# Attention stage of an encoder step: when stream keys and bias rows are asked for, and how many first splits precede the first job

## The chip, the cores and the metric

The program runs on one core of one Trainium2 chip. The metric is the device time of one execution, in microseconds (us); lower is better. A core has TensorE (PE: matmuls and transposes, with its weight loads as PEld), VectorE (DVE), ScalarE (ACT), GpSimd (POOL) and SyncE (SP, which here issues nearly all DMAs). Each engine works through its own instructions in order and waits on semaphores for others.

## The reference, cut to what matters

One layer over a prompt of 2048 tokens and over eight running streams of 16 new tokens each, model width 1024, 8 heads of 64 in group A ("fox") and 8 in group B ("band"):

```python
h = rmsnorm(x, norm_mix_pre)
qa, ka, va, logf, qb, kb, vb = project_in(h, w_in, b_forget)
oa = fox_fn(qa, ka, va, logf)      # causal, logit += C[t] - C[s], C = cumsum(logf)
ob = band_fn(qb, kb, vb)           # own chunk of 64 and the 8 before, bias by distance
oa = rmsnorm(oa.reshape(...), gain_out_a)
ob = rmsnorm(ob.reshape(...), gain_out_b)
x = x + rmsnorm(jnp.concatenate([oa, ob], axis=-1) @ w_out, norm_mix_post)
hf = rmsnorm(x, norm_ffn_pre)
x = x + rmsnorm((jax.nn.silu(hf @ w_gate) * (hf @ w_up)) @ w_down, norm_ffn_post)
```

For a stream, group A attends to 1024 cached keys and values and the 16 new ones, group B to 512 cached ones and the new ones. Everything is float32.

## The kernel before, in words

The program has four stages, one after the other: `front` (norm and input projection), `attend`, `mix_out` (output projection) and `feed_forward`. The change touches `attend` alone. All dense products are made of high and low parts (a high part that the matmul takes exactly, and the rest), so a raw block of queries or keys is first split: ACT writes the high part (`split_high`, L1083 on), DVE the low part (`split_low`, L1139 on).

**Jobs.** The stage is a list of 144 jobs (`JOBS`). Jobs 0 to 63 are group A of the prompt: four pairs of heads, 16 query blocks of 128 each, block i against i+1 key tiles. From job 64 (`WIDE`) on come four pairs of group B, 16 blocks each with at most five key tiles, and among them 16 stream jobs, one behind the third of every four band jobs: streams 0 to 7 are group A of the eight running streams (nine key tiles), 8 to 15 group B (five). A stream job thus comes every fifth job: n, n+5, and so on.

**Order.** `attend_order` writes out one order for PE, ACT and DVE: the scores of job n+2 stand among the transposes ("turns") of job n. A job goes: PE scores, in pieces, to two score buffers; DVE adds the bias to a piece and keeps the running minimum (`biased`, L1234; for streams L1203), which frees the score buffer; ACT takes the exponential (L1106); PE transposes (L999, streams L979); ACT and DVE copy out (L1117, L1245); PE multiplies with the values (L1035, streams L1015); DVE copies (`outward`), PE transposes back, DVE normalises (`evict`, L1276), SP stores (L780, streams L777).

**The pair's queries and keys.** A pair has eight raw chunks of 128 x 512, 256 KB each: four of keys (c below 4) and four of queries. They go through three raw buffers; SP asks for chunk x (`load_raw`, L755) when the low split of chunk x-3 has freed the buffer. For pairs 1 to 7 the chunks are asked during jobs 2 to 9 of the pair before and split after jobs 4 to 11. For pair 0, ACT and DVE make all eight splits before the first job, and PE's job 0 waits for the eighth low split (L950). On SP the first three chunks come first, then the two bias rows of the pair (L768, 1 MB each), its values (L761, 1 MB), then the other five chunks, then the bias table of group B (L836, L840), then the loop over jobs.

**Stream constants.** DVE's `stream_consts` (L1150 on) waits for GpSimd's steps on `own` and `fold`, and stands ahead of DVE's first low split. `own` lies in `sx[2][:, 0, 0:512]`, which job 2 overwrites.

**Streams on SP.** Keys of group A come in two halves of 1 MB to `kr[0]` and `kr[1]` (L799), which is the space of the prompt's bias rows `bb[0]`; values likewise to `bb[1]` (L822). The bias rows of a group A stream, `bt[s % 2]` (0.5 MB, L803), are broadcast from `csum`; GpSimd then adds a mask to their last 16 columns (L914), and DVE's first biased piece of the stream waits for that. Group B has one table for all streams (L809). SP's loop does, for each job n, in this order: values and bias rows of the next pair at i = 2 and 3; the queries, keys, bias rows and values of stream 0 at job 64; keys and bias rows of the next stream at a stream job; values of the next stream at the job after it; the store of job n-1 (which waits for its evict); and a raw chunk.

```python
if n == WIDE:
    load_queries()
    load_keys(0)
    load_values(0)
if n in STREAM_AT and p + 1 < NST:
    load_keys(p + 1)
if n - 1 in STREAM_AT and JOBS[n - 1][1] + 1 < NST:
    load_values(JOBS[n - 1][1] + 1)
if n >= 1:
    store(n - 1)
if kind != "stream" and p + 1 < NPAIR and 2 <= i < 10:
    load_raw(8 * (p + 1) + i - 2)
```

A piece of a stream's scores waits for its half of the keys, and from the third piece on (the 16 new keys) for the biased first piece, since two score buffers alternate (L933).

Of the kernel before, what the change touches and what calls it, by code (L numbers as in the profile page):

```python
# [15 lines left out]
SEQ = 2048  # L16
# [623 lines left out]
def attend(nc, t, keep, neg_c):  # L640
# [6 lines left out]
    LMAX = PAST_A + NQ  # L647
    WIDE = PAIR_AT[NPAIR // 2]
    NPT, NSX, NSM, NOS, NRAW = 3, 3, 5, 4, 3
    HALVES = [(s, h) for s in range(NST) for h in range(stream_keys(s) // 4)]  # L650
# [12 lines left out]
    with ExitStack() as ctx:  # L663
# [38 lines left out]
        qb = [sx[2][:, 1, 5 * P + 2 * GW + P * u:5 * P + 2 * GW + P * (u + 1)].rearrange("p (c q) -> p c q", c=CH) for u in range(2)]  # L702
        own = sx[2][:, 0, 0:GW]

# [22 lines left out]
        def splits_at(n):  # L727

            kind, p, i = JOBS[n]
            return [8 * (p + 1) + i - 4] if kind != "stream" and p + 1 < NPAIR and 4 <= i < 12 else []  # L730

        def last_of(n, g):
            return g == len(job_groups(n)) - 1
# [11 lines left out]
        with nc.Block() as block:  # L745

            @block.sync
            def _(sp):
                def load_raw(x):
                    p, c = divmod(x, 8)  # L750
                    base, off = rows(p)
                    r0 = base + off + (GW if c < 4 else 0)
                    if x >= NRAW:
                        sp.wait_ge(s_lo, x - NRAW + 1)
                    sp.dma_start(raw[x % NRAW][:], t["zT"][r0:r0 + P, (c % 4) * 512:(c % 4 + 1) * 512]).then_inc(s_raw[x % NRAW], 16)  # L755
# [33 lines left out]
                def load_keys(s):  # L789
                    band, b = divmod(s, NB)  # L790
                    keys = t["cache_bk"] if band else t["cache_ak"]
                    for h in range(stream_keys(s) // 4):
# [3 lines left out]
                        else:  # L796
                            ps, ph = HALVES[x - 2]
                            sp.wait_ge(s_sc, S0[STREAM_AT[ps]] + ph + 1)
                        sp.dma_start(kr[x % 2], keys[b][:, :, h * 512:(h + 1) * 512]).then_inc(l_k[x % 2], 16)  # L799
                    if band == 0:  # L800
                        if s >= 2:
# [39 lines left out]
                for n in range(NJOB):  # L841
                    kind, p, i = JOBS[n]
                    if kind != "stream" and p + 1 < NPAIR:
                        if i == 2:
                            load_v(p + 1)
                        if i == 3 and fox(p + 1):
                            load_bias(p + 1)
                    if n == WIDE:
                        load_queries()
                        load_keys(0)  # L850
                        load_values(0)
                    if n in STREAM_AT and p + 1 < NST:
                        load_keys(p + 1)
                    if n - 1 in STREAM_AT and JOBS[n - 1][1] + 1 < NST:
                        load_values(JOBS[n - 1][1] + 1)
                    if n >= 1:
                        store(n - 1)
# [59 lines left out]
            def _(pe):  # L917
# [19 lines left out]
                def score(n, g):  # L937
# [10 lines left out]
                    diag = fox(p) and tiles[-1] == i  # L948
                    if i == 0:
                        pe.wait_ge(s_lo, 8 * (p + 1))  # L950
# [131 lines left out]
            def _(act):  # L1082
                def split_high(x):  # L1083
                    p, c = divmod(x, 8)
                    u = p % 2
# [33 lines left out]

                for x in range(8):  # L1120
                    split_high(x)
                for e in range(2):
                    exps(0, e)
                for what, n, g in ORDER:
                    if what == "turn":
# [7 lines left out]
                        if last_of(n, g):  # L1133
                            for x in splits_at(n):
                                split_high(x)

            @block.vector
            def _(dve):
                def split_low(x):  # L1139
                    p, c = divmod(x, 8)  # L1140
                    u = p % 2
# [141 lines left out]
                nc.vector.drain().then_inc(s_cst, 1)  # L1283
                stream_consts()
                for x in range(8):
                    split_low(x)
                held, ended = [], []
                for what, n, g in ORDER:
                    if what == "score":
                        biased(n, g)  # L1290
                    else:
# [13 lines left out]
                        copy(n, g)  # L1305
                        held.append((n, g))
                        if n == WIDE and g == 0:
                            stream_pad()
# [966 lines left out]
```

## Time and profile before

| | |
|---|---|
| median of 3 executions | 3291.67 us (3288.47 to 3296.19) |
| the profiled execution | 3288.23 us, span 3286.5 us |
| PE busy | 2942.9 us (90%) |
| DVE, ACT, POOL busy | 1659.4, 1208.5, 469.6 us |
| mean granted TensorE clock | 0.96 |
| attention stage | about 610 to 1480 us of the span |
| keys of group A streams, asked to landed | 1024 KB each, 8.3 us (median) |
| DMA traffic | 376.37 MB, mean 115 GB/s |

The span is from the first to the last instruction. A timeline row gives the start, the length, the engine, the line of the kernel and the tiles, and in brackets how long the engine was idle before and what released it. A window row gives a stretch "A:B" in us and its length, then the busy time of PE, PEld, DVE, ACT and POOL in it (with the number of instructions), the granted clock (1.00 is 2.4 GHz, 0.50 is 1.2 GHz), the share of time that the 16 DMA engines were busy, and the GB/s moved.

### The profile page before, as it was taken

What the parts mean: (1) busy time and instruction counts of PE and PEld (TensorE: products, weight loads), DVE (VectorE), ACT (ScalarE), POOL (GpSimd) and SP (SyncE); (2) the same over time, 40 slices, a digit from 0 to 9 for tenths busy, and PEclk for the clock granted to TensorE, in tenths of its full rate; (3) what the DMA queues carried; (4) which work ended last, traced back from release to release, by engine and by line L of the source; (5) the groups of instructions that cost most, each with busy time, mean ns of one, the idle gap of its engine ahead of it and who ended that gap; (6) DMA issues with size and microseconds to landing.
All of it is one profiled execution on the core that took longest, in us unless ns stands there. A gap on an engine that the chain in (4) does not pass through costs nothing. (4 is left out here: it accounts for less than half of the span.)

```text
span 3286.5 us, 57063 instructions
## 1 busy us (share of the span) xinstructions
PE 2942.9 (90%) x23073; PEld 2633.0 (80%) x23073; DVE 1659.4 (50%) x3253; ACT 1208.5 (37%) x2124; POOL 469.6 (14%) x402
## 2 busy tenths in 40 slices
PE   7999999688888667787994999999999996998998
PEld 7999999577677445655884999999999994886887
DVE  6222221377666445664445766786676653223444
ACT  5320000266666344553443333433343333223211
POOL 0000000100000000000113544453344320000000
PEclk9999999899999789998996999999999998999999
DMA  5322121412211765434543322333222225434553
GB/s 166 89 78 76 63 72 60 137 39 76 74 36 46 211 201 181 145 112 167 162 141 118 141 104 103 122 107 105 105 87 105 105 79 164 106 93 135 176 176 118
DMA packets 275868, 376.37 MB, mean 115 GB/s; under 512 B 16456, under 2 KB 203864, under 8 KB 263576
## 3 DMA queue, kind: packets, MB, share of 16 engines
q1 hardware_dynamic: 273368, 368.43, 35.3%
q8 instruction: 184, 3.01, 0.4%
q10 hardware_dynamic: 2240, 4.30, 0.4%
q14 instruction: 76, 0.62, 0.1%
HBM read 283.52 MB, written 89.15 MB: 113 GB/s over the span
## 5 line engine op out<-in xcount | busy, mean ns | idle before, releaser
L2064 PE MATMUL dwn_py<-dwn_wh,dwn_ah 128*128 128x512 f32 x748 | 296.9, 397 | 42.0 <-DVE dwn_al L2139 32.6
L1117 ACT ACTIVATE att_pts<-att_pt 128x384 f32<-128x384 f32 (+3 forms) x444 | 207.7, 493 | 284.6 <-PE att_pt L999 255.6
L2065 PE MATMUL dwn_py<-dwn_wl,dwn_ah 128*128 128x512 f32 x748 | 294.1, 393 | 0.0
L2066 PE MATMUL dwn_py<-dwn_wh,dwn_al 128*128 128x512 f32 x748 | 293.9, 393 | 0.0
L1106 ACT ACTIVATE att_sx<-att_sx,att_nm 128x640 f32<-128x640 f32 (+17 forms) x272 | 265.2, 976 | 19.0 <-DVE att_os L1276 17.7
L1035 PE MATMUL att_po<-att_pts,att_vv 128*64 128x128 f32 x3296 | 230.0, 286 | 44.0 <-DVE att_os L1276 38.2
L1035 PEld LDWEIGHTS att_po<-att_pts,att_vv 128*64 128x64 f32 x3296 | 195.0, 144 | 66.2 <-issue 62.1
L999 PEld LDWEIGHTS att_pt<-att_eye,att_sx 64*128 64x128 f32 x3296 | 132.2, 141 | 130.8 <-ACT att_pts L1117 83.1
L79 PE MATMUL frt_pz<-frt_xhi,frt_hi 128*128 128x448 f32 (+1 forms) x640 | 230.5, 360 | 0.0
L81 PE MATMUL frt_pz<-frt_xhi,frt_lo 128*128 128x448 f32 (+1 forms) x640 | 230.5, 360 | 0.0
L80 PE MATMUL frt_pz<-frt_xlo,frt_hi 128*128 128x448 f32 (+1 forms) x640 | 230.1, 359 | 0.0
L999 PE MATMUL att_pt<-att_eye,att_sx 64*128 64x64 f32 x3296 | 171.3, 234 | 65.1 <-ACT att_pts L1117 33.7
L514 DVE TENSOR_TENSOR frt_shared<-frt_pz,frt_rb 128x448 f32<-128x448 f32 (+1 forms) x80 | 48.9, 611 | 313.6 <-PE frt_pz L81 313.6
L2064 PEld LDWEIGHTS dwn_py<-dwn_wh,dwn_ah 128*128 128x128 f32 x748 | 142.3, 190 | 80.6 <-DVE dwn_al L2139 33.7
L79 PE MATMUL frt_pv<-frt_hi,frt_xhi 128*128 128x256 f32 (+1 forms) x544 | 157.2, 289 | 18.6 <-DVE frt_lo L446 15.7
L1779 PE MATMUL gup_z<-gup_hh,gup_wh 128*128 128x362 f32 (+1 forms) x528 | 173.2, 328 | 0.0
L1781 PE MATMUL gup_z<-gup_hl,gup_wh 128*128 128x362 f32 (+1 forms) x528 | 173.2, 328 | 0.0
L1782 PE MATMUL gup_z<-gup_hh,gup_wl 128*128 128x362 f32 (+1 forms) x528 | 172.7, 327 | 0.0
L2066 PEld LDWEIGHTS dwn_py<-dwn_wh,dwn_al 128*128 128x128 f32 x748 | 142.3, 190 | 30.1
L2065 PEld LDWEIGHTS dwn_py<-dwn_wl,dwn_ah 128*128 128x128 f32 x748 | 142.5, 190 | 28.4
L1713 POOL TENSOR_TENSOR gup_tr<-gup_wr 128x512 f32<-128x512 f32 x66 | 88.9, 1347 | 523.7 <-DVE gup_wl L1884 410.1
L80 PE MATMUL frt_pv<-frt_lo,frt_xhi 128*128 128x256 f32 (+1 forms) x544 | 154.3, 284 | 0.0
(251 smaller groups left out, 7473.7 us busy)
## 6 DMA issues: line engine op xcount, KB each, us to landing
gup_wr<-in_w_gu SPq DMA_DIRECT2D x65, 1024.0 KB, 5.1
dwn_ar<-mid_act SPq DMA_DIRECT2D x67, 704.0 KB, 6.0
att_raw<-out_zT SPq DMA_DIRECT2D x64, 256.0 KB, 3.0
att_bb<-in_cache_ak SPq DMA_DIRECT2D x16, 1024.0 KB, 8.3
att_bb<-in_cache_av SPq DMA_DIRECT2D x16, 1024.0 KB, 14.2
mid_act<-gup_ao SPq DMA_DIRECT2D x44, 362.0 KB, 2.5
out_zT<-frt_shared SPq DMA_DIRECT2D x64, 224.0 KB, 1.9
frt_raw<-in_w_slab SPq DMA_DIRECT2D x11, 1024.0 KB, 5.3
```

The costliest lines, as they stand in the source:

```text
L79: nc.tensor.matmul(out, a_hi(k), b_hi(k), start=(k == 0), stop=False)
L80: nc.tensor.matmul(out, a_hi(k), b_lo(k), start=False, stop=False)
L81: last = nc.tensor.matmul(out, a_lo(k), b_hi(k), start=False, stop=(k == kk - 1))
L999: last = nc.tensor.transpose(pt[x][:, to:to + 64], sx[n % NSX][r, e, c:c + P], eye[r, r])
L1035: last = nc.tensor.matmul(po[n % 2][r, 0:P], vv[u][:, kt, r], pts[G % NPT][:, e, j, :], start=(g == 0 and j == 0), stop=(g == len(groups) ...
L1106: nc.scalar.activation(sx[n % NSX][:, e, :w], sx[n % NSX][:, e, :w], ACT.Exp, bias=nm[n % NSX][:, e:e + 1], scale=-1.0, accum_out=sums[n % ...
L1117: nc.scalar.activation(pts[G % NPT][:, :, 0:k, 64 * x:64 * x + 64], pt[x][:].rearrange("p (e j q) -> p e j q", e=2, q=64)[:, :, 0:k, :], A ...
L1779: nc.tensor.matmul(out, high[:, k, :], hh[:, x, k, :w], start=(k == 0 and not more), stop=False, skip_group_check=True)
L1781: nc.tensor.matmul(out, high[:, k, :], hl[:, x, k, :w], start=False, stop=False, skip_group_check=True)
L2064: nc.tensor.matmul(out, ah[u][:, j, :], wh[:, j, :], start=(j == 0), stop=False)
L2065: nc.tensor.matmul(out, ah[u][:, j, :], wl[:, j, :], start=False, stop=False)
L2066: last = nc.tensor.matmul(out, al[u][:, j, :], wh[:, j, :], start=False, stop=(j == NJ - 1))
```

## The change

Six edits, all in `attend`:

- Keys of a stream are asked at the job before the stream job ahead of it (one job sooner), those of stream 0 at job 63 in place of 64.
- The bias rows get a function of their own, `load_table`; those of streams 0 and 1 are asked at job 64 behind the queries, those of stream s+2 at the job after stream s, behind the values of stream s+1.
- The raw chunks of every pair are taken in the order keys 0, queries 0, keys 1, queries 1 and so on (`CHUNKS`).
- Only two chunks are split before job 0; ACT and DVE split two more behind each of jobs 0, 1 and 2 (`first_splits`).
- PE's wait for the low splits of pair 0 is now made in fours: job 0, 4, 8 and 12 wait for 2, 4, 6 and 8 of them.
- `stream_consts` moves behind the first group of job 6 on DVE, and `own` to columns 1536 to 2047 of the second half of `sx[2]`, which no job before 14 writes.

```diff
+    CHUNKS = [0, 4, 1, 5, 2, 6, 3, 7]
-        own = sx[2][:, 0, 0:GW]
+        own = sx[2][:, 1, SEQ - GW:]
+        def first_splits(n):
+            return [2 * n + 2, 2 * n + 3] if n < 3 else []
@@ load_raw, split_high, split_low @@
-                    p, c = divmod(x, 8)
+                    p, c = x // 8, CHUNKS[x % 8]
@@ sync: load_keys, load_table @@
+                def load_table(s):
+                    band, b = divmod(s, NB)
                     if band == 0:
                         if s >= 2:
                             sp.wait_ge(s_bi, 2 * S0[STREAM_AT[s - 2] + 1])
...
+                    if n == WIDE - 1:
+                        load_keys(0)
                     if n == WIDE:
                         load_queries()
-                        load_keys(0)
+                        load_table(0)
+                        load_table(1)
                         load_values(0)
-                    if n in STREAM_AT and p + 1 < NST:
-                        load_keys(p + 1)
+                    if n + 1 in STREAM_AT and JOBS[n + 1][1] + 1 < NST:
+                        load_keys(JOBS[n + 1][1] + 1)
                     if n - 1 in STREAM_AT and JOBS[n - 1][1] + 1 < NST:
                         load_values(JOBS[n - 1][1] + 1)
+                        if JOBS[n - 1][1] + 2 < NST:
+                            load_table(JOBS[n - 1][1] + 2)
@@ tensor: score @@
-                    if i == 0:
+                    if p == 0 and i % 4 == 0:
+                        pe.wait_ge(s_lo, 2 * (i // 4 + 1))
+                    if p > 0 and i == 0:
                         pe.wait_ge(s_lo, 8 * (p + 1))
@@ scalar @@
-                for x in range(8):
+                for x in range(2):
                     split_high(x)
...
                         if last_of(n, g):
-                            for x in splits_at(n):
+                            for x in first_splits(n) + splits_at(n):
                                 split_high(x)
@@ vector @@
-                stream_consts()
-                for x in range(8):
+                for x in range(2):
                     split_low(x)
...
                         held.append((n, g))
+                        for y in first_splits(n):
+                            split_low(y)
+                        if (n, g) == (6, 0):
+                            stream_consts()
```

## Rows read from the trace of the kernel before

**Rows 1.** Waits of all engines, 590 to 1490 us: total, times, longest.

```profile
PE att_s L956 <- DVE att_ql L1147: 25.2, 1, 25.2
...
PE att_s L933 <- DVE att_nm L1203: 20.8, 8, 4.4
...
PE att_s L933 <- DMA att_bb<-in_cache_ak: 20.2, 7, 7.2
...
ACT att_qh L1093 <- DMA att_raw<-out_zT: 18.2, 5, 8.1
```

**Rows 2.** Timeline of the start: start us, us, engine, line, operation, tiles [idle before].

```profile
611.59 0.91 SPq L768 DMA_DIRECT2D att_bb<-mid_neg_c  x2
...
618.60 0.17 DVE L1152 MEMSET att_fc<- 128x128 f32 x1 [4.15 <-POOL att_fold L900]
...
620.72 1.90 DVE L1145 TENSOR_TENSOR att_kl<-att_raw,att_kh 128x512 fp32r<-128x512 f32 x3
...
621.43 6.95 SPq L755 DMA_DIRECT2D att_raw<-out_zT  x5
...
626.02 0.63 ACT L1091 ACTIVATE att_kh<-att_raw 128x512 fp32r<-128x512 f32 x1 [9.18 <-DMA att_raw<-out_zT]
...
633.88 0.29 DVE L1234 CUSTOM_DVE_ANT_0 att_sx<-att_s,att_bb 128x128 f32<-128x128 f32 x1 [1.51 <-PE att_s L962]
```

**Rows 3.** DMA issues from 609 to 613 us: KB each, median us to landing.

```profile
att_bb<-mid_neg_c SPq DMA_DIRECT2D x2, 1024.0 KB, 8.7
...
att_vv<-out_v SPq DMA_DIRECT2D x1, 1024.0 KB, 12.8
```

**Rows 4.** Timeline about streams 0 and 1, the columns as in rows 2.

```profile
1052.46 0.32 SPq L780 DMA_DIRECT2D mid_mixT<-att_os  x1
...
1063.42 1.27 SPq L799 DMA_DIRECT2D att_bb<-in_cache_ak  x2
...
1064.73 0.73 SPq L803 DMA_DIRECT2D att_sx<-mid_csum  x1
...
1080.54 0.22 POOL L914 TENSOR_TENSOR att_sx<-att_sx,att_late 128x16 f32<-128x16 f32 x1 [443.84 <-DMA att_sx<-mid_csum]
...
1090.96 0.43 SPq L761 DMA_DIRECT2D att_vv<-out_v  x1
...
1097.60 1.25 SPq L799 DMA_DIRECT2D att_bb<-in_cache_ak  x2
...
1107.54 1.45 PE L933 MATMUL att_s<-att_bb,att_sx 128*32 128x512 f32 x8 [2.88 <-DMA att_bb<-in_cache_ak]
```

**Rows 5.** Windows of scoring streams 0, 1, 4, 5, 7; sum of 1 to 7.

```profile
1064.20:1081.99 17.79, 4.18 (x28) 0.74 (x28) 2.04 (x9) 1.85 (x6) 0.22 (x1) 0.58 0.99 285
...
1103.59:1113.60 10.01, 3.67 (x38) 1.35 (x40) 1.28 (x4) 2.81 (x7) 0.22 (x1) 0.72 1.05 286
...
1192.58:1200.90 8.32, 2.44 (x28) 0.65 (x32) 0.89 (x3) 1.52 (x6) 0.22 (x1) 0.76 1.00 272
...
1221.23:1231.77 10.54, 4.16 (x38) 1.42 (x40) 1.33 (x4) 2.31 (x6) 0.22 (x1) 0.64 1.05 245
...
1290.97:1294.45 3.48, 2.70 (x42) 1.09 (x40) 1.26 (x4) 2.19 (x6) 0.22 (x1) 1.00 1.06 325
...
sum 48.75, PE 21.30 PEld 7.77 DVE 8.56 ACT 16.95 POOL 1.54; mean PE 3.04 PEld 1.11 DVE 1.22 ACT 2.42 POOL 0.22
```

**Rows 6.** Windows: streams 0 to 8, and four stretches between streams.

```profile
1081.99:1311.48 229.49, 167.06 (x2534) 121.45 (x2533) 118.19 (x457) 106.26 (x264) 1.54 (x7) 0.86 0.65 192
...
1113.60:1140.07 26.47, 21.63 (x310) 17.11 (x311) 15.47 (x60) 12.64 (x30) 0.00 (x0) 0.78 0.52 163
...
1146.26:1171.87 25.61, 20.13 (x310) 15.85 (x310) 16.04 (x61) 12.12 (x29) 0.00 (x0) 0.88 0.58 177
...
1231.76:1257.51 25.75, 20.20 (x311) 15.93 (x311) 15.46 (x60) 13.20 (x32) 0.00 (x0) 0.88 0.56 175
...
1264.07:1290.97 26.90, 20.57 (x310) 15.89 (x310) 16.04 (x61) 12.12 (x29) 0.00 (x0) 0.81 0.56 177
```

More of the change, by code:

```diff
@@ L1083, in split_high @@
                 def split_high(x):
-                    p, c = divmod(x, 8)
+                    p, c = x // 8, CHUNKS[x % 8]
                     u = p % 2
@@ L1139, in split_low @@
                 def split_low(x):
-                    p, c = divmod(x, 8)
+                    p, c = x // 8, CHUNKS[x % 8]
                     u = p % 2
```

## The prediction

> **What bounds the kernel now.** I read the waits of the TensorE queue (PE) over the attention stage first, because PE is the engine that is nearly always at work and its waits say which stalls are long and rare. Three lines stand out [rows 1]: one wait of 25.2 us for the low half of the last query split, eight times the scores of a stream wait for the reduced minimum of the piece before (20.8 us), and seven times they wait for a stream's keys (20.2 us). The rest of PE's waits are short ones between jobs. The change is aimed at these three, so the sum goes over these three places, each read in its own timeline.
>
> The start [rows 2]: the vector engine (DVE) can do no low split until it has built the constants of the streams, and those wait for GpSimd: it goes idle for 4.15 us, starts the constants at 618.60 and the first low split at 620.72. The raw buffers are free only then, so SyncE (SP) asks for the other five chunks from 621.43 on, and the first of them reaches ScalarE (ACT) at 626.02. PE starts behind the last of them, the first biased scores at 633.88. The two bias rows of the first pair (asked at 611.59) land a median of 8.7 us after their issue, and the values after 12.8 us [rows 3].
>
> The first stream [rows 4]: a store is issued at 1052.46, the keys only at 1063.42 and the table of bias rows at 1064.73, behind 2 MB of keys. GpSimd gets the table at 1080.54, and the last piece is scored at 1081.99. PE had left its band work at 1064.20; the window between holds 17.79 us and 4.18 us of matmuls [rows 5].
>
> The next seven streams of group A [rows 5]: the windows from the first key matmul (or the start of the wait for it) to the end of the last piece sum to 48.75 us; those of streams 1, 4, 5 and 7 stand there. The seventh, without a late transfer, takes 3.48 us. The DMA share is 1.00 to 1.06 in them, and 0.52 to 0.58 in the stretches between [rows 6]: transfers stand behind each other just where they are waited for.
>
> The clock [rows 6]: over the 229.5 us from the end of the first stream's scores to the first stream of group B PE was granted 0.86 of full speed, though nothing but the stalls differs: the 3.48 us window has 1.00, the 10.54 us window 0.64.
>
> **The change, part by part.**
>
> (A) First splits. ACT and DVE do two of eight before job 0. DVE's first low split can follow its two casts of constants; PE's scores then wait for nothing but these, at about 616. But the biased step also needs the bias rows, 611.59 and half a microsecond for the second, and 8.7: 620.8. The pipeline so starts 633.88 - 620.8 = 13.0 us sooner. Given back: six splits now stand in ACT's queue, two behind each of jobs 0 to 2, ahead of the next job's copies, which PE waits for. Each takes 0.63 us, so 3.8 us if nothing hides them. The fourth chunk, now asked at about 615, still stands behind the values on SP's one queue; values land at about 625.4, so the chunk at about 626, as now [rows 2, 3], while ACT would come to it near 624.6: 1.4 us more. The later chunks are each asked when a low split frees a buffer, and fit in the same steps. DVE's six low splits (0.69 us each) lie beside ACT's. I take 5.0; bounds 0 (all in the slack of these small jobs) and 11 (ACT's 3.8, DVE's 4.1 and a further 3 of waits for chunks). Moved to job 6: the constants, 620.72 - 618.60 = 2.1 us of DVE; I take half of that on the path, 1.0, bounds 0 and 2.1. The table and far loads of group B come after the eighth chunk, needed 400 us later: nothing. Stores of jobs 0 to 3 wait a little behind them; four output buffers cover that. (A) = 13.0 - 5.0 - 1.0 = 7.0.
>
> (B) First stream. Its keys are asked behind the store at 1052.46, 10.9 us sooner, and have all landed when PE needs them. The queries still wait for the turn of the last group A job and stay where they are; the table goes right behind them, without the 2 MB ahead. No row shows such a table alone. From below, a raw chunk of half the size is used 4.6 us after it was asked [rows 2]; from above, this table took 15.8 us [rows 4]. The nearest rows are the bias rows, broadcast from memory in the same way at twice the size, 8.7 us with chunks before them [rows 3]; at 0.5 MB and with 1 MB of queries partly ahead I take 6, so it lands at 1070. From its landing to the end of the last piece is 1081.99 - 1080.54 = 1.45 us, so the stream's scores end at 1071.5 instead of 1081.99: 10 us (bounds 1 and 12).
>
> (C) Streams 1 to 7. Tables come a whole stream period ahead and can't be late. Keys are asked one job sooner, just behind the store before: for stream 1 right behind the values of the next pair, 1090.96 + 0.5 instead of 1097.60 [rows 4], 6 us sooner. The second half of its keys landed at about 1107.5 [rows 4], so it now comes at 1102 to 1103, delayed a little by the 1 MB in front, against a need one piece (about 1 us) behind 1103.59, less the 1 to 2 us by which the jobs before run faster. Streams 1 and 5 have those values in front; I leave 1.5 us of waits to the two. All seven at the clean 3.6: 48.75 - 25.2 = 23.6, less 1.5: 22 (bounds 18 and 24).
>
> (D) The clock. 229.5 x 0.14 = 32 us of full clock are lost. The three slow scoring windows hold 10.01 x 0.28 + 8.32 x 0.24 + 10.54 x 0.36 = 8.6 of that, which (C) counts already; 23 lie between streams. What they cost I read from two pairs of equal stretches of jobs [rows 6]: 26.47 us at 0.78 against 25.75 at 0.88 is 0.72 us for 2.7 lost, and 26.90 at 0.81 against 25.61 at 0.88 is 1.29 for 2.0: 0.26 and 0.63 us each. At 0.4 it is 9.2; an eighth of it stays for the first stream, which still stalls: 8.0 (bounds 3 and 14). The granted clock is a mix of 1.2 and 2.4 GHz (0.64 to 0.76) in the windows with late transfers, and 2.4 GHz throughout in the one without [rows 5]. The Trainium skill (TensorE: Matmul & The Clock Gate, HAM oscillation) prices a cold stretch at throttled time times one half, so one microsecond for each lost here; by it (D) would be some 20 and the sum 59. The pairs speak against it, because PE waits for ACT and DVE in much of a job and these don't slow down.
>
> (E) No gain: streams 8 to 15. They have half the keys and no wait for them in any row; a sooner request changes nothing. SP meets one wait earlier, for the scores of the stream at hand before the next keys; those are done well before the store ahead of it, so nothing queues behind it.
>
> Sum: 7 + 10 + 22 + 8 = 47 us. The profiled execution took 3288.23 us (span 3286.5), 3.4 below the median of the three, 3291.67. So 3241 for an execution like the profiled one, and 3244.7 against the median: **3245**.
>
> **The rivals.**
>
> R1, the clock pays in full: with the stalls gone PE's steps are the path and each lost microsecond counts one. (D) is 20, the time 3291.7 - 59 = 3233. For it: PE is busy 167 of the 229 us [rows 6]. Against: both pairs. 0.12.
>
> R2, transfers stay in line: the askings are sooner, the landings are not. DMA share 1.04 in each scoring window, on one queue. The waits for keys of streams 1 to 7 stay (of 20.2 us stream 0 has the longest, 7.2, and some more; 10.5 are theirs), half the clock with them (4), and the start pays back what it gained, since its six chunks stand behind 3 MB (7). 47 - 21.5: 3266. Against: between the windows the share is little over half, so an earlier request has room. The Trainium skill (DMA: Bandwidth & Descriptors, Queues, rings and completion order) says that each DMA engine consumes descriptors in ring order; by that, what is asked behind the next pair's values lands behind them, which is this rival. 0.14.
>
> R3, slower: raw chunks behind keys. For three pairs, the chunks of the third and the seventh job are now asked behind 2 MB of keys, and ACT does its splits in order, ahead of copies that PE waits for. ACT's longest wait for a chunk of queries is 8.1 us now, of 18.2 us in five waits [rows 1]. Six such waits of 8.1 are 49 us: the gain is gone, 3293; if the following chunk of each is held by 1.5 more it is 3302. It decides only if each is held over 7.8 us, and a split comes about two jobs, 10 us, after its request. 0.04.
>
> R4, it doesn't do what it says: SP comes to the moved lines no sooner, because the store ahead of them is the late one and every part but the tables falls flat; that is between R2 and no change. 0.03, at 3280.
>
> **How the numbers follow.** Forecast 0.67, R1 0.12, R2 0.14, R3 0.04, R4 0.03. The forecast's own bounds: (A) 0 to 13, (B) 1 to 12, (C) 18 to 24, (D) 3 to 14 would be 22 to 63; they are unlikely to go one way, so 35 to 59 for it: 3233 to 3257. With R1 inside and most of R2: range 3229 to 3266. A measurement of this kernel tells about 0.2% (6.6 us) from no change. Slower by more: R3's upper half and a bit of the unseen, 0.03. Within: 0.03. Faster: 0.94.
>
> **What would show it.** First biased scores at 620 to 622 and job 3 some 7 us sooner than before; the single PE wait of 25 us down to about 12. The waits for the reduced minimum fall from 20.8 to about 8, those for keys from 20.2 to under 3, GpSimd's add for stream 1 on comes many microseconds ahead of DVE. The clock is 1.00 in every window of rows 5 and above 0.95 between. Wrong: ACT waits for raw chunks of over 3 us in groups; keys of streams 1 and 5 still waited for by more than 2 us each; or the clock still 0.5 after streams 1 to 7.

## The result, and where the time went

The changed kernel takes 3267.99 us, median of four runs (3266.86 to 3269.07), the kernel before 3293.02 beside it (four runs, 3288.47 to 3296.19): a ratio of 0.9925, 95% interval 0.9908 to 0.9942. That is 25 us (19 to 30) where 47 were forecast; 3245 was said, and the range ended at 3266. The two profiled executions took 3288.23 and 3266.86, spans of 3286.5 and 3265.1, so the traces show 21.4 of the 25.

The waits of all engines of the changed kernel, 590 to 1490 us (total, times, longest), answer to [rows 1]:

```profile
ACT att_kh L1105 <- DMA att_raw<-out_zT: 115.3, 8, 91.2
...
PE att_pt L1013 <- ACT att_pts L1131: 53.8, 35, 7.5
ACT att_qh L1107 <- DMA att_raw<-out_zT: 39.4, 10, 7.7
...
PE att_s L970 <- DVE att_ql L1161: 9.5, 1, 9.5
PE att_s L970 <- DVE att_nm L1248: 8.6, 11, 3.4
...
PE att_s L945 <- DVE att_nm L1217: 5.5, 1, 5.5
```

The three waits that the change is aimed at fell as forecast or further: the one for the low splits from 25.2 to 9.5, those for the reduced minimum from 20.8 to 5.5, those for a stream's keys from 20.2 to none. In their place stand PE's waits for ACT's copies of the transposes (L1131), which were 33.7 us in 33 waits before, none over 2.6, and are 53.8 now with one of 7.5, and PE's waits for the minimum of a prompt job's piece (L1248), 8.6 for 1.5. ACT's waits for raw chunks did not grow as a whole. Those for chunks of queries went from 18.2 to 39.4, but the chunks now come in another order, so keys and queries have to be taken together: without the one wait of 91 us for the stage ahead they are 68.9 us before and 63.5 now. The line of the keys before, which [rows 1] does not show:

```profile
ACT att_kh L1091 <- DMA att_raw<-out_zT: 142.1, 13, 91.4
```

The windows that answer to [rows 5] (streams 0, 1, 4, 5, 7), then the whole stretch from stream 0 to stream 8 and three stretches between streams, as in [rows 6]:

```profile
1071.45:1079.23 7.78, 2.24 (x26) 0.69 (x28) 0.93 (x3) 0.29 (x2) 0.22 (x1) 0.83 0.88 187
1099.63:1102.68 3.05, 2.63 (x38) 1.06 (x40) 1.88 (x5) 1.74 (x5) 0.00 (x0) 1.00 1.05 397
1185.60:1189.30 3.70, 3.66 (x30) 0.99 (x32) 0.70 (x2) 1.21 (x5) 0.00 (x0) 0.52 1.05 397
1210.60:1213.20 2.60, 2.60 (x42) 1.06 (x38) 1.61 (x4) 1.82 (x5) 0.00 (x0) 1.00 1.05 390
1273.50:1276.20 2.70, 2.70 (x42) 1.12 (x40) 1.67 (x4) 1.36 (x4) 0.00 (x0) 1.00 1.09 404
```

```profile
1079.20:1292.50 213.30, 159.88 (x2532) 116.27 (x2532) 117.82 (x456) 105.82 (x262) 1.54 (x7) 0.89 0.67 212
1102.68:1132.76 30.08, 19.72 (x312) 15.29 (x313) 14.91 (x58) 14.18 (x34) 0.22 (x1) 0.83 0.59 196
1135.40:1164.00 28.60, 19.50 (x314) 15.16 (x318) 15.62 (x61) 13.63 (x33) 0.22 (x1) 0.88 0.58 169
1213.20:1243.30 30.10, 19.25 (x319) 14.92 (x318) 15.17 (x60) 14.21 (x34) 0.22 (x1) 0.89 0.64 186
```

Streams 1 to 7 are scored in 3.0, 2.6, 2.6, 4.4, 2.6, 2.6 and 2.6 us by the trace, 20.4 in all against 48.75; stream 0's window, from PE's last band work to the last piece, has 9.3 us against 17.8. Both terms were met. But the stretch between streams 1 and 2 grew from 26.47 to 30.08 us, that between 2 and 3 from 25.61 to 28.60, that between 5 and 6 from 25.75 to 30.10, with the same matmuls in them and the clock no higher than 0.89.

**The account.** The end of each job's evict in the two traces, after minus before, gives it in stages: at job 4, -1.5 us (where the forecast had -7); at job 62, the last but one of group A, +5.6, so 7.2 lost (forecast none); at job 63, behind stream 0's scores, -3.5, so 9.2 gained (forecast 10); at job 110, past streams 1 to 8, -20.0, so 16.5 gained (forecast 22 + 8); at the last job -21.9. Of the 1.5 us at job 4 the stage ahead has 0.7: the pair's bias rows are asked that much sooner. Three things are to be explained: the 13.5 missing among the streams, the 5.5 missing at the start, and the 7.2 lost in group A.

**Among the streams.** This is SP's queue about stream 1 in the changed kernel, by the timeline (columns as in [rows 2]), and the split that ACT makes of the chunk asked at 1101.16, then PE's next transposes:

```profile
1087.42 0.44 SPq L765 DMA_DIRECT2D att_vv<-out_v  x1
1087.90 2.88 SPq L803 DMA_DIRECT2D att_bb<-in_cache_ak  x2
...
1092.82 1.29 SPq L759 DMA_DIRECT2D att_raw<-out_zT  x1
...
1094.68 1.40 SPq L829 DMA_DIRECT2D att_bb<-in_cache_av  x2
...
1097.78 0.64 SPq L810 DMA_DIRECT2D att_sx<-mid_csum  x1
...
1101.16 0.42 SPq L759 DMA_DIRECT2D att_raw<-out_zT  x1
```

```profile
1111.37 0.63 ACT L1107 ACTIVATE att_qh<-att_raw 128x512 fp32r<-128x512 f32 x1 [7.15 <-DMA att_raw<-out_zT]
```

```profile
1112.32 0.91 PE L1013 MATMUL att_pt<-att_eye,att_sx 64*128 64x64 f32 x12 [7.23 <-ACT att_pts L1131]
```

The chunk takes 10.2 us from its request to its use, behind 2 MB of values and 0.5 MB of bias rows; ACT stands before its split for 7.15 us with the copies that PE needs behind it, and PE stands 7.23. The same happens behind streams 2, 5 and 6 (ACT 5.97, 7.66, 5.42). The kernel before had four such waits as well (6.91, 6.22, 4.46, 8.14); the one behind stream 1 has the same 10.2 us from request to use:

```profile
1108.19 0.42 SPq L755 DMA_DIRECT2D att_raw<-out_zT  x1
```

```profile
1118.45 0.63 ACT L1091 ACTIVATE att_kh<-att_raw 128x512 fp32r<-128x512 f32 x1 [6.91 <-DMA att_raw<-out_zT]
```

Yet PE's waits for ACT's copies in the stretch from stream 0 to stream 8 were 9.1 us before and are 25.9 now:

```profile
PE att_pt L999 <- ACT att_pts L1117: 9.1, 4, 2.6
```

```profile
PE att_pt L1013 <- ACT att_pts L1131: 25.9, 5, 7.5
```

ACT's own waits for chunks in it grew only from 25.8 us to 30.4. What changed is when they fall. Before, PE's stall in the stream's scores gave the chunk time to travel: the four chunks came 4.9, 5.0, 5.0 and 5.7 us after the stream's last score, and PE had work for most of that. Now they come 8.7, 7.5, 9.2 and 7.0 us after it.

### The profile page after: what moved, and what is told of

Its sections match the earlier page's. It is cut to its first block and busy times, and to the rows that moved or that the text cites. A ratio compares the mean times of both kernels' runs of the same rounds, so it can differ in the third digit from the quotient of the medians.

```text
span 3265.1 us, 57072 instructions
## 1 busy us (share of the span) xinstructions
PE 2937.8 (90%) x23073; PEld 2632.7 (81%) x23073; DVE 1661.9 (51%) x3253; ACT 1208.4 (37%) x2124; POOL 470.6 (14%) x402
## 5 line engine op out<-in xcount | busy, mean ns | idle before, releaser
L1131 ACT ACTIVATE att_pts<-att_pt 128x384 f32<-128x384 f32 (+3 forms) x444 | 207.7, 493 | 256.6 <-PE att_pt L1013 227.7
L1013 PE MATMUL att_pt<-att_eye,att_sx 64*128 64x64 f32 x3296 | 171.1, 234 | 88.2 <-ACT att_pts L1131 53.8
```

What stands on the lines that cost most here:

```text
L1013: last = nc.tensor.transpose(pt[x][:, to:to + 64], sx[n % NSX][r, e, c:c + P], eye[r, r])
L1131: nc.scalar.activation(pts[G % NPT][:, :, 0:k, 64 * x:64 * x + 64], pt[x][:].rearrange("p (e j q) -> p e j q", e=2, q=64)[:, :, 0:k, :], A ...
```

## The experiments

Fourteen more runs were made, one of them the changed kernel again, each beside the kernel before on the same chip, which took 3292.6 to 3293.5 us there. All kernels compute the whole reference. The edits are to the kernel before or to the changed one, as each says; times are medians of four or more runs where an interval stands.

**The two halves apart.** e1_streams is the kernel before with the edits to SP's loop alone, e2_start the changed kernel with the old loop, the reverse of the same lines:

```diff
+                    if n == WIDE - 1:
+                        load_keys(0)
                     if n == WIDE:
                         load_queries()
-                        load_keys(0)
+                        load_table(0)
+                        load_table(1)
                         load_values(0)
-                    if n in STREAM_AT and p + 1 < NST:
-                        load_keys(p + 1)
+                    if n + 1 in STREAM_AT and JOBS[n + 1][1] + 1 < NST:
+                        load_keys(JOBS[n + 1][1] + 1)
...
+                        if JOBS[n - 1][1] + 2 < NST:
+                            load_table(JOBS[n - 1][1] + 2)
```

> The kernel before with the stream edits alone (keys a job sooner, bias rows two streams ahead); the start as before. Theory T (the stream edits are worth more than the whole change, the start edits cost time by the end of group A): the changed kernel's last group A jobs come 4 to 6 us late although its first job is evicted 3 us early, so without the start edits 25 + 4 = 29 us are gained: 3264. Rival (the late group A jobs are chance, another phase of the clock, and the start is worth its 2 to 3 us): 3271.

> The changed kernel with the old requests for keys and bias rows: only the start edits are left (two splits before the first job, the order of the chunks, the constants at job 6). Theory T: 3 us gained at the first evict, lost again by 1.3 us at job 4 to 6 and by 1 to 3 us in each of three pairs; 0 to 5 us slower than before: 3293 to 3298. Rival: 2 to 3 us faster, 3290. My prediction had 7 us faster, 3286.

e1: 3263.43 us, ratio 0.9901 [0.9886, 0.9916]. e2: 3296.47, twelve runs, ratio 1.0001 [0.9991, 1.0011]. The stream edits carry the whole gain (30 us), and the start edits give nothing that the runs can tell from zero, though they take 15.7 us from PE's one long wait (9.5 in e2 as in the changed kernel).

**Values behind the chunk.** In e3_raw_first the values of the next stream and the bias rows are asked behind the store and the raw chunk of the same job:

```diff
-                    if n - 1 in STREAM_AT and JOBS[n - 1][1] + 1 < NST:
-                        load_values(JOBS[n - 1][1] + 1)
-                        if JOBS[n - 1][1] + 2 < NST:
-                            load_table(JOBS[n - 1][1] + 2)
...
                         load_raw(8 * (p + 1) + i - 2)
+                    if n - 1 in STREAM_AT and JOBS[n - 1][1] + 1 < NST:
+                        load_values(JOBS[n - 1][1] + 1)
+                        if JOBS[n - 1][1] + 2 < NST:
+                            load_table(JOBS[n - 1][1] + 2)
```

> The changed kernel with SP's requests for the next stream's values and the table of the one after it put behind the store and the raw chunk of the same job. Theory T (the raw chunk asked behind 2 MB of values and 0.5 MB of table lands 10 us after its request, ACT stands at its split for 6 to 8 us in four jobs, and PE with it: 7.2, 5.8, 7.5 us and one more): the four waits go, 15 to 20 us faster than the changed kernel: 3250, and the low clock behind each wait with them. Rival (the chunk is asked late by SP in any case, or another transfer takes the place of the values): 3268.

3272.75 us, ratio 0.9937 [0.9921, 0.9953]: no better than the change, 5 us worse by the medians. The chunk in question now came 3.3 us after its request, and the wait went to the next one, asked at 1097.14 and used at 1109.66, 12.5 us, with ACT waiting 9.56 of them. Waits of e3, 1079 to 1300 us:

```profile
ACT att_kh L1105 <- DMA att_raw<-out_zT: 45.8, 6, 9.8
PE att_pt L993 <- ACT att_pts L1131: 27.0, 4, 8.2
```

At stream 5, moreover, PE waited 4.1 us and once more 1.2 us for keys, which it did not in the changed kernel. A stream period of group A asks for 4.5 MB of keys, values and bias rows on one queue; whichever small chunk stands behind a block of them is the late one. Moving the order within the queue only picks it.

**Bias rows alone, keys alone.** e5_tables is the kernel before with the bias rows asked two streams ahead and the keys as they were, e6_keys with the keys asked a job sooner and the bias rows as they were:

```diff
@@ e5, to e1 @@
-                    if n == WIDE - 1:
-                        load_keys(0)
                     if n == WIDE:
                         load_queries()
+                        load_keys(0)
...
-                    if n + 1 in STREAM_AT and JOBS[n + 1][1] + 1 < NST:
-                        load_keys(JOBS[n + 1][1] + 1)
+                    if n in STREAM_AT and p + 1 < NST:
+                        load_keys(p + 1)
@@ e6, to e1 @@
-                        load_table(1)
...
+                    if n in STREAM_AT and p + 1 < NST:
+                        load_table(p + 1)
...
-                        if JOBS[n - 1][1] + 2 < NST:
-                            load_table(JOBS[n - 1][1] + 2)
```

> The kernel before with the bias rows two streams ahead alone; keys asked where they were, the start as before. Streams 1 to 7 were scored in 48.9 us before and in 20.4 after the change; the waits for keys hold 10.5 of the 28.5. Theory T: about 18 us of the windows go and 3 at stream 0, less some 5 for raw chunks that are now waited for behind values and table: 3277. Rival (bias rows alone do it, the keys then being on time because the bias rows are out of their way): the windows sum to 22 or less, 3266.

> The kernel before with the keys a job sooner alone; each stream's bias rows asked where they were, at the stream job before. The bias rows then have no keys ahead of them on the queue and should land 7 us after their request instead of 13. Theory T: they come just in time for most streams, windows sum to 25 to 30 us, and the raw chunk behind values is waited for as in the changed kernel: 3268 to 3272. Rival (keys alone gain only the 10.5 us of key waits, the table stays the last to land): windows near 38, 3282.

e5: 3279.94, ratio 0.9959 [0.9943, 0.9975]. e6: 3259.59, ratio 0.9899 [0.9884, 0.9914]. Together (e1) they give 30, keys alone 33 (more than either theory said), bias rows alone 13; the difference of e1 and e6 is within their intervals. Windows of scoring streams 1, 4 and 5 in e6:

```profile
1101.40:1109.10 7.70, 3.10 (x42) 1.11 (x40) 1.36 (x4) 3.27 (x8) 0.22 (x1) 0.87 1.04 242
1182.40:1186.10 3.70, 3.46 (x32) 0.92 (x32) 0.86 (x3) 1.41 (x5) 0.22 (x1) 0.57 1.05 387
1206.00:1215.30 9.30, 2.97 (x40) 1.00 (x38) 1.27 (x4) 3.27 (x8) 0.22 (x1) 0.87 1.05 241
```

Without the early bias rows streams 1 and 5 are still late, 5 and 7 us over a clean window; and yet e6 is as fast as e1. The waits tell why: the chunk that is late comes beside or soon behind that stall, as in the kernel before. PE's waits for ACT's copies are 10.1 us in six in e6, 25.2 in four in e5 (1085 to 1300 us), while ACT's waits for chunks are 28.0 us in both. So the bias rows two ahead take a stall away and uncover another.

**The chunks on another queue.** If the shared queue is the cause, the chunks must come in time from a queue of their own. In e7_raw_act, the changed kernel, ACT asks for the chunks of pairs 1 to 7 itself (the same transfer, issued by ACT), one job ahead of its split and behind the split made in that job:

```diff
-                    if kind != "stream" and p + 1 < NPAIR and 2 <= i < 10:
-                        load_raw(8 * (p + 1) + i - 2)
@@ scalar, behind the splits of job n @@
+                            if kind != "stream" and p + 1 < NPAIR and 3 <= i < 11:
+                                load_raw(8 * (p + 1) + i - 3)
```

> The changed kernel with the raw chunks of pairs 1 to 7 asked on ACT's own DMA queue, one job before their split, in place of SP's queue. Theory T (a chunk is late because it stands in SP's queue behind 2 MB of values, 0.5 MB of bias rows or 2 MB of keys): each chunk lands 3 to 5 us after its request even beside them, ACT waits no more than 1 to 2 us for any, PE's waits for ACT's copies of 7.2, 5.8 and 7.5 us go: 15 to 20 us faster than the changed kernel, 3250. Rival (the 16 DMA engines are shared and full for these 10 us, so the queue makes no difference): waits as before, 3268.

3236.26 us, ratio 0.9827 [0.9812, 0.9842]: 57 us under the kernel before. The whole stretch and the ones between streams 1 and 2, 2 and 3, 5 and 6, 6 and 7 in e7, then its waits, 1071 to 1261 us:

```profile
1071.10:1260.80 189.70, 155.01 (x2532) 112.67 (x2532) 117.69 (x456) 106.03 (x262) 2.16 (x7) 0.95 0.73 236
1095.20:1121.00 25.80, 20.12 (x314) 15.68 (x317) 15.11 (x60) 14.23 (x34) 0.22 (x1) 0.87 0.72 229
1123.60:1146.20 22.60, 17.57 (x310) 13.47 (x310) 15.62 (x61) 13.64 (x33) 0.75 (x1) 1.00 0.68 212
1192.00:1216.80 24.80, 19.05 (x314) 14.76 (x318) 15.08 (x60) 14.12 (x34) 0.22 (x1) 0.93 0.75 244
1219.40:1241.90 22.50, 17.91 (x314) 13.56 (x314) 15.63 (x61) 13.64 (x33) 0.31 (x1) 1.00 0.66 218
```

```profile
ACT att_kh L1110 <- DMA att_raw<-out_zT: 13.1, 4, 4.5
PE att_pt L991 <- ACT att_pts L1136: 6.1, 3, 2.8
```

The stretch is 23.6 us shorter than in the changed kernel and 39.8 shorter than before; PE's busy time in it fell from 159.88 to 155.01 with the same 2532 matmuls, which is the clock, 0.95 against 0.89. The DMA share is higher (0.73 against 0.67), but that is the same traffic in a shorter stretch (236 GB/s over 189.7 us and 212 GB/s over 213.3 us are both about 45 MB). The requests of the chunk behind stream 1 and of the one after it, then the split of the latter:

```profile
1090.20 0.33 ACTq L1100 DMA_DIRECT2D att_raw<-out_zT  x1
...
1096.69 0.34 ACTq L1100 DMA_DIRECT2D att_raw<-out_zT  x1
1104.25 0.63 ACT L1110 ACTIVATE att_kh<-att_raw 128x512 fp32r<-128x512 f32 x1 [4.50 <-DMA att_raw<-out_zT]
```

The Trainium skill (DMA: Bandwidth & Descriptors, Queues, rings and completion order) says that descriptors of one queue are consumed in ring order on each DMA engine and that an engine goes round robin between the queues it has work for; both halves agree with these traces: the chunk that takes 10.2 us behind 2.5 MB on SP's queue was asked at 1090.20 on ACT's, 2.5 us behind the same values, landed after 6.5 us, some 4 us ahead of the second half of those values, and was used at 1096.68 without a wait. The chunks are not free of the bulk even so: with nothing large under way one takes 2.7 us, and the next one took 7.6 (asked 1096.69, used 1104.25, 4.50 of it waited); ACT waits as long once more, 4.28 us behind stream 5.

Two things keep e7 from being a clean test of the queue. The edit also moves the request some 3.5 us ahead against the stream's scores. By the numbers of this one chunk the two have about equal parts in the 7.15 us wait that went: 3.5 us by the sooner request, 3.7 by the sooner landing; that is worked out and not tested, and no run parts the two. And the gain is not all in this place. Of the 36.9 us between the profiled executions of e7 and of the changed kernel, 26.9 lie between jobs 63 and 110 by the ends of the evicts, and 7.8 between jobs 4 and 62, where no stream is: there, too, ACT waited for chunks, 18.3 us before and 20.7 in the changed kernel, and not at all in e7. That is part of why e7 came out 14 us under what its theory said.

**The same on other kernels.** f1_act_old_start is e1 with this edit, f4_act_keys_only e6 with it; f2_act_start_eight is e8 (below) with it:

> The stream edits with the start of before, and the raw chunks of pairs 1 to 7 on ACT's queue. Theory T with its size for the start (the start edits are worth the 2.8 us of the first evict less the 1.3 us that the constants cost at job 6): 1 to 2 us slower than the changed kernel with chunks on ACT's queue (3236.3), 3238. Rival (the start edits lose by the end of group A even now): the same or faster, 3232 to 3236.

> Keys a job sooner, the bias rows still asked at the stream job before, the start of before, raw chunks on ACT's queue. With the chunks out of SP's queue the bias rows two streams ahead cost nothing any more, so only their gain is left. Theory T: the windows of streams 1 and 5 are 5 and 6.7 us longer as in the run with keys alone, with the clock behind them 12 to 15 us slower than its pair with bias rows ahead (3238): 3251. Rival (bias rows are in time in any case once SP's queue has fewer chunks): 3238.

> As the run before it, with all eight splits first, the constants at job 6 and the first pair's values behind its chunks. Theory: first evict 2.6 us sooner than in the kernel before and 1.3 lost at job 6, as with two splits first: 3236 to 3237, so how the splits are placed is worth nothing against moving the constants. Rival (two splits first are better, the low clock apart): 3240.

f1: 3231.37, ratio 0.9814 [0.9796, 0.9832]. f4: 3239.62, 0.9833 [0.9817, 0.9849]. f2: 3233.52, 0.9816 [0.9800, 0.9833]. With the chunks out of the way the bias rows two ahead seem to pay: f1 is 8 us under f4 by the medians (the theory said 12 to 15, the rival 0, and the intervals overlap), where e1 was 4 over e6. And f1, with the old start, is 5 under e7, again by the medians: the change's start shows no worth here either.

**The start: eight splits first.** e8_start_eight is e1 with all eight splits ahead of job 0, but with the constants at job 6, `own` moved as in the change, and pair 0's values asked behind its chunks:

```diff
-                stream_consts()
                 for x in range(8):
                     split_low(x)
...
                 load_bias(0)
-                load_v(0)
                 for x in range(NRAW, 8):
                     load_raw(x)
+                load_v(0)
```

> The stream edits with another start: all eight first splits still before job 0, in the old order, but the stream constants at job 6, and the first pair's values asked behind its chunks. Theory S (the start before was held by DVE waiting for GpSimd's constants, and the changed start loses what it gains because splits stand between jobs 0 to 2): first biased scores near 629 instead of 633.9, nothing lost afterwards: 4 to 5 us faster than the stream edits alone (3263.4), 3259. Rival (the first bias rows and chunks share the DMA engines, so the eighth chunk comes no sooner): no change, 3263.

3260.83 us, ratio 0.9903 [0.9886, 0.9921], the same as e1. The first biased piece stands at 630.85, 9.4 us later than in the changed kernel, and yet job 3 is evicted at the same distance from the pair's first request for bias rows, 44.8 us in e8 and 44.7 in the changed kernel. What the change gains at the first piece it has lost by job 3. (That request comes at 611.59 in the trace of before and at 610.9 to 615.6 in the others, by the stage ahead, so times of the start are best counted from it.)

**The start: a copy of GpSimd's.** In the changed kernel the eighth low split took 3.23 us, and GpSimd's copy ran beside it:

```profile
633.46 0.69 DVE L1159 TENSOR_TENSOR att_kl<-att_raw,att_kh 128x512 fp32r<-128x512 f32 x1 [0.83 <-ACT att_kh L1105]
634.06 3.23 DVE L1161 SCALAR_TENSOR_TENSOR att_ql<-att_raw,att_qh 128x512 fp32r<-128x512 f32 x1
```

```profile
633.65 3.10 POOL L916 COPY att_brel<-att_far 128x3072 f32<-128x3072 f32 x1 [15.22 <-DMA att_far<-in_rel_bias]
```

e4_copy_later makes the copy wait for the eight low splits (`pool.wait_ge(s_lo, 8)` ahead of it); it is needed only by group B, 400 us later.

> The changed kernel with GpSimd's 2.85 us copy of the far biases waiting until the last first low split is done. Theory L (DVE's low split of 3.23 us, 0.68 us elsewhere, was held by GpSimd's copy running beside it): that split takes 0.7 us, and 2 to 2.5 us are gained: 3265.5. Rival (the split is long for another reason, or what follows absorbs it): the split stays long, or the time stays 3268.

3264.94 us, ratio 0.9908 [0.9892, 0.9924]: 3 us less by the medians, within the intervals. The trace is plain: 

```profile
638.34 0.68 DVE L1162 SCALAR_TENSOR_TENSOR att_ql<-att_raw,att_qh 128x512 fp32r<-128x512 f32 x1
...
639.29 0.42 DVE L1249 CUSTOM_DVE_ANT_0 att_sx<-att_s,att_bb 128x256 f32<-128x256 f32 x1
```

```profile
639.20 2.74 POOL L917 COPY att_brel<-att_far 128x3072 f32<-128x3072 f32 x1 [16.09 <-DVE att_ql L1162]
```

The split is back at 0.68, and job 0 is evicted 28.5 us after the pair's first request, against 31.4 in the changed kernel and 33.6 before. f3_act_copy_later has this edit and e7's:

> The changed kernel with raw chunks on ACT's queue, and GpSimd's copy of the far biases behind the last first low split. Theory L: DVE's sixth first low split takes 0.7 us in place of 3.2, first evict 2.5 us sooner after the first biased piece, 2 us faster in all: 3234. Rival (the low clock at the start gives it back): 3236.

3229.54 us, ratio 0.9803 [0.9787, 0.9820], 7 under e7 by the medians; job 0 evicted after 28.8.

**The start: VectorE's order.** g2_low_behind is f3 with DVE's first low splits of job n moved from ahead of the biased pieces of job n+2 to behind them:

```diff
+                        if n >= 2 and g == score_count(n) - 1:
+                            for y in first_splits(n - 2):
+                                split_low(y)
...
-                        for y in first_splits(n):
-                            split_low(y)
```

> f3_act_copy_later with one more edit: the low splits of the first jobs stand in VectorE's order behind the biased pieces of the same job's scores, not ahead of them. Theory (what the start gave back was VectorE's order: biased pieces standing behind low splits that wait for ScalarE's high splits): the wait of TensorE for a biased piece in jobs 0 to 2 (9.5 us in the profile of the changed kernel) falls to a few us, the evictions of jobs 0 to 2 come 3 to 5 us sooner, and the time is about 3226.5. Rival (the start is held by ScalarE, and by TensorE's own clock): the low splits were late because ScalarE was, so the biased pieces come no sooner than TensorE can use them, or the later keys are late by as much: 3228 to 3231, no change.

3225.19 us, ratio 0.9801 [0.9777, 0.9825], the fastest of all, 68 us under the kernel before: the time forecast (3226.5), but its runs (3222.3 to 3233.9) don't part it from f3. The trace does: job 0 is evicted 25.4 us after the request, 3.4 sooner than in f3, and job 3 after 37.1 against 41.9, 9.8 sooner than before. The expectation was wrong in its first number: the 9.5 us are PE's wait for the low splits of the two chunks ahead of job 0, which did not move, and they stay. PE's waits for the minimum of a biased piece, which the edit aims at, were 5.6 us up to 655 us in the changed kernel and 3.2 in f3, and are gone.

```profile
PE att_s L969 <- DVE att_ql L1170: 9.5, 1, 9.5
```

**The changed kernel again.** g1_after_again is the changed kernel, one more execution:

> The changed kernel once more, unchanged, for its profile. Theory (the drift of about 7 us between jobs 3 and 62 of the first half is chance, low clock spells that fall on other jobs each time): the evictions of job 61 stand at another distance from those of the kernel before than the +4.1 of the first profile, by some us, and the steps of +1 to +2 at jobs 19, 35, 51 and 62 stand elsewhere or have other sizes. Rival (the start edits cause it): the same steps at the same jobs, and the same +4 at job 61.

3263.56 us. From job 4 to job 62 this execution lost 4.2 us against the kernel before, the first one 7.2, and the steps differ: at job 19 one stands at -1.1, the other at +0.5 (from -1.0 and -1.5 at job 4), at job 62 at +3.2 and +5.6. So some 3 us of it is chance; the granted clock from 660 to 1060 us was 0.99 before, 0.97 in the first execution and 0.98 in this one. e2 and e3, with the same start, lost 1.2 and 0.9, e4 4.2, and e8, with its own start, 5.1; kernels with the old start and the chunks on SP's queue (e1, e5, e6) lost 1.3, -0.6 and 1.2. Neither theory has it all: the first overstated the chance, the rival the sameness. Whether a loss of a few microseconds belongs to the start edits stays open.

## Why the prediction was wrong

**What bounds the kernel** was read rightly for the streams: the gain is where two of the three long waits were, and the stream edits gave all of it. The third, at the start, was taken away as well and gave nothing by the end of group A.

**(A), first splits, 7.0: wrong in one term.** The pipeline started when it was said to: first biased piece at 621.50, for 620.8 forecast. The term "given back, 5.0" was mis-sized: counted from the pair's first request the first piece is 11.7 us sooner (22.3 to 10.6) and job 0's evict 2.2 (33.6 to 31.4), so 9.5 went. Of them GpSimd's copy has 2.9 (31.4 to 28.5 in e4; 2.3 from e7 to f3, 31.1 to 28.8), the low splits ahead of the biased pieces in DVE's order 3.4 (28.8 to 25.4 in g2), and 3.2 are left to the rest, ACT's six splits and the chunks, which is below the 5.0 that I gave to them. The prediction costed DVE's low splits as lying "beside ACT's": their 0.69 us did, but DVE works in order, so each biased piece behind them waited until ACT had come to its high split. And it named no engine that shares anything with DVE. The constants at job 6 cost 1.3 (the step from -2.8 to -1.5 at job 4), for 1.0 forecast. So 0.9 us were left of the 7.0, and by the whole time nothing: e2 equals the kernel before.

**(B), first stream, 10: right**, 9.2 measured. Its bias rows were asked at 1069.1 and used by GpSimd at 1077.7, 8.7 us, not 6; the window still lost 8.5.

**(C), streams 1 to 7, 22: right in itself**, 28.4 in the windows (48.75 to 20.4), because a clean window is 2.6 us at full clock and not 3.5. The early keys were in time and so were the bias rows.

**(D), clock, 8, and the term that is missing beside it: the step that failed.** The sum took each stall away by itself and asked of the moved requests only whether they would land in time. What is late behind the bulk, and what the stalls hid, it put at nothing: the raw chunks appear in R3 alone, and only behind keys. It also read ACT's waits for chunks from the line of the queries, 18.2 us; that of the keys had 50.7 more, the wait for the stage ahead left out. A raw chunk behind the values and the bias rows of the job after a stream was late before and after the change; before, PE's stall for the stream used up much of the chunk's travel, and with that stall gone PE waits nearly in full, 25.9 us for 9.1, that is 16.8 more, against the 13.5 missing. With each such wait the clock fell, so the clock's 32 us of [rows 6] went only to 23 (213.3 x 0.11). The prediction's own sign of being wrong, waits of ACT for raw chunks of over 3 us in groups, is what came. e7 bears it out: with the chunks on a queue of their own and asked sooner, PE's waits for ACT's copies fell to 7.3 us in that stretch (6.1 and 1.2 at two lines of transposes), and the gain was 57 us in place of 25. That is more than the shortfall of 22, because e7 also frees chunks that were late before the change.

**The rivals.** R3 had this mechanism, a chunk behind megabytes on SP's queue with ACT standing ahead of copies, with a chance of 0.04 and the wrong cargo: it named the keys, and e6, with the keys a job sooner and nothing else, is by the medians the fastest of the kernels that leave the chunks on SP's queue. The bias rows, which the prediction called safe, are part of the cargo: with them moved and the keys not (e5) PE waits 25.2 us for ACT's copies, with the keys alone (e6) 10.1. R2 gave nearly the measured time (3266), but by luck, from a cause that is not there: the stream's keys and bias rows did land sooner. Its ring order is real, for the chunks. R1, the clock in full, isn't borne out: from the changed kernel to e7 the stretch lost 23.5 and 9.5 us of clock (213.3 x 0.11, 189.7 x 0.05), 14 less, and PE's busy time fell by 4.9.

**The range** missed by 2 us; its lower bounds took each term alone, and no term stood for a wait uncovered.

## What to carry to other kernels

When a stall of the busiest engine is taken away, list the waits of the other engines that overlapped it or followed it closely: they come to the surface, and the gain is the stall less what it covered. On a queue that works in order, ask of each request that is moved or left what stands ahead of it after the move, above all for small transfers with a near deadline; here they did best on another engine's queue than the bulk (e7, f1 to f4). In engines that work in order, put work whose input is late (a split of a chunk still to be made by another engine) behind the work that someone is waiting for.

## What was not expected of the hardware

- A GpSimd copy of 128x3072 in SBUF and DVE's low split of 128x512 (two SBUF inputs) held each other: 3.23 us for the split, 0.68 alone, and 3.10 for the copy, 2.74 alone. Beside DVE's biased piece, with one input in PSUM, the same copy took 2.74 and the piece 0.42 as ever. The Trainium skill (SBUF — State Buffer, SBUF: two separate sides) describes the two engines' shared ports as an exclusive lock for a whole instruction; the split, which started 0.4 us into the copy and ended 0.5 us after it, agrees.
- A small request on ACT's queue overtook the bulk on SP's: 256 KB asked 2.5 us behind the first of 2 MB of values landed after 6.5 us in e7, while the second megabyte took 12.7; on SP's queue, behind the same bytes, it took 10.2. With nothing large under way 256 KB took 2.6 to 2.8 us on either queue.
- In each stretch of 28 to 30 us that holds one stall of 5 to 8 us near its start, PE's granted clock averages 0.83 to 0.89, a mix of 1.2 and 2.4 GHz; the stretches between streams 2 and 3 and 6 and 7 without such a stall have 1.00 in e7, and those with a stall of 2.8 and 2.5 us behind streams 1 and 5 have 0.87 and 0.93.
